# A gated-attention and pooling trunk: attention's input product as 24 steps of seven products, half of x turned beside them, W_out's sums moved into mixing

## What is computed

```python
h = x @ w_in                                   # 2048 x 1024 by 1024 x 3088
q, k, v, g, lr = split(h, [512, 1024, 2048, 3072])
gk = log_sigmoid(lr @ w_gk + b_gk) / 16        # lr: 16 columns
b = cumsum(gk within a chunk)
qe, ke, kd = q * exp(b), k * exp(-b), k * exp(b_last - b)
o = tril(qe @ ke.T) @ v + qe @ S               # S: state, decayed per chunk
o = rms_norm(o) * norm_w * silu(g)
x = layernorm(ALPHA * x + o @ w_out)
# layer 1: u, z = x @ w_in; m = (pool(u) - u) @ w_grp + b; x = layernorm(ALPHA * x + (m * scale * silu(z)) @ w_out)
```

## Time and profile before

| | us |
|---|---|
| median of three runs | 2002.89 |
| the profiled execution | 2001.48 |
| its span in the profile | 1999.6 |
| prepare | 0 to 132.3 |
| project, first to last matmul | 135.3 to 690.7 |
| attention | 692.8 to 1002 |
| mixing, with its first turns from 1009 | to 1999.6 |

### The profile page before, as it was taken

One profiled execution on the slowest core, in us unless ns is written; L12 is line 12 of the kernel. 1 busy time (PEld: TensorE's weight loads), 2 busy tenths in 40 slices (PEclk: granted clock), 3 DMA queues, 4 the chain that ended last, 5 costly groups with the idle time before them and its releaser, 6 DMA issues.

```text
span 1999.6 us, 24456 instructions
## 1 busy us (share of the span) xinstructions
PE 1914.5 (96%) x8974; PEld 1588.5 (79%) x8974; DVE 1161.7 (58%) x1539; ACT 701.3 (35%) x1065; POOL 431.5 (22%) x268
## 2 busy tenths in 40 slices
PE   8999999999999989999949999999999999999997
PEld 7778887888888778888738888887888886787786
DVE  4330102332415277787675688868678657546998
ACT  4441213131313243343354444344434335224331
POOL 0005200000000000000043666423334343322430
PEclk9999999999999999999979999999999999999999
DMA  8766530334233464455322444333322225647342
GB/s 254 221 202 239 178 103 17 108 87 118 79 101 87 159 242 164 172 187 170 136 96 74 153 141 152 135 104 137 129 88 73 94 74 193 249 170 272 129 177 95
DMA packets 229912, 287.74 MB, mean 144 GB/s; under 512 B 17216, under 2 KB 170176, under 8 KB 227904
## 3 DMA queue, kind: packets, MB, share of 16 engines
q1 hardware_dynamic: 225216, 278.20, 42.0%
q10 hardware_dynamic: 4608, 8.39, 1.1%
HBM read 186.93 MB, written 99.61 MB: 143 GB/s over the span
## 4 chain that ended last, share of the span: by engine, by line
PE 41%; DVE 4%; issue 4%; ACT 1%; POOL 0%; DVEq 0%; POOLq 0%; ACTq 0%
PE banks L165 13%; PE banks L166 13%; PE banks L167 13%; DVE m_w_lo L1922 1%; DVE m_x_lo L1936 1%; ACT m_x_hi L1728 0%; DVE m_x_lo L1914 0%; PE banks L1621 0%; PE banks L1668 0%; DVE m_stats L2025 0%; DVE m_x_lo L1896 0%; DVE m_res L2019 0%; DVE m_res L2035 0%; POOL m_s L1859 0%; DVE m_win_b L1968 0%
## 5 line engine op out<-in xcount | busy, mean ns | idle before, releaser
L165 PE MATMUL banks<-m_x_hi,m_w_hi 128*128 128x512 f32 x1320 | 517.6, 392 | 9.4 <-DVE m_res L2019 3.5
L166 PE MATMUL banks<-m_x_lo,m_w_hi 128*128 128x512 f32 x1320 | 515.3, 390 | 0.0
L167 PE MATMUL banks<-m_x_hi,m_w_lo 128*128 128x512 f32 x1320 | 515.0, 390 | 0.0
L165 PEld LDWEIGHTS banks<-m_x_hi,m_w_hi 128*128 128x128 f32 x1320 | 248.7, 188 | 63.7 <-DVE m_w_lo L1922 10.0
L166 PEld LDWEIGHTS banks<-m_x_lo,m_w_hi 128*128 128x128 f32 x1320 | 248.8, 188 | 52.0 <-issue 0.7
L167 PEld LDWEIGHTS banks<-m_x_hi,m_w_lo 128*128 128x128 f32 x1320 | 248.7, 188 | 52.0
L1854 POOL TENSOR_TENSOR m_s<-pair_raw 128x512 f32<-128x512 f32 x24 | 47.3, 1969 | 891.6 <-POOLq L947 757.5
L165 PE MATMUL banks<-x_hi,h_w_hi 128*128 128x512 f32 x512 | 199.9, 390 | 0.8 <-DVE h_g_out L833 0.8
L166 PE MATMUL banks<-x_lo,h_w_hi 128*128 128x512 f32 x512 | 199.3, 389 | 0.0
L167 PE MATMUL banks<-x_hi,h_w_lo 128*128 128x512 f32 x512 | 199.3, 389 | 0.0
L1716 ACT ACTIVATE m_w_hi<-m_s 128x512 fp32r<-128x512 f32 x184 | 115.5, 629 | 202.7 <-PE banks L167 179.2
(11 more groups left out here) (220 smaller groups left out, 3117.7 us busy)
## 6 DMA issues: line engine op xcount, KB each, us to landing
p_in<-in_pool_w_in SPq DMA_DIRECT2D x32, 256.0 KB, 4.9
p_rows<-in_x SPq DMA_DIRECT2D x16, 512.0 KB, 5.2
w_fused<-p_out SPq DMA_DIRECT2D x32, 256.0 KB, 3.9
h_out_rows<-in_pool_w_out SPq DMA_DIRECT2D x16, 512.0 KB, 6.7
v_tiles<-v_out ACTq DMA_DIRECT2D x32, 256.0 KB, 2.1
w_terms<-h_out_terms SPq DMA_DIRECT2D x8, 1024.0 KB, 5.6
h_raw<-in_gla_w_in SPq DMA_DIRECT2D x16, 512.0 KB, 4.2
g_tiles<-h_g_out SPq DMA_DIRECT2D x32, 256.0 KB, 2.3
```

The costliest lines, as they stand in the source:

```text
L165: nc.tensor.matmul(out, a_hi, b_hi, start=first, stop=False, skip_group_check=True)
L166: nc.tensor.matmul(out, a_hi, b_lo, start=False, stop=False, skip_group_check=True)
L167: return nc.tensor.matmul(out, a_lo, b_hi, start=False, stop=last, skip_group_check=True)
```

## The change

`project` becomes 24 steps of seven products, with the order of mixing. Steps 0 to 7 form v for two token tiles at a time: the stationary quarters are tiles of x, loaded from a new DRAM copy of x turned (`x_in`), the moving ones the seven terms of v's weights (`b_hi`, `b_lo`). Steps 8 to 15 and 16 to 23 form q with k, or a pair of gate columns, for the first and the second half of the tokens; there the moving terms are the seven terms of x. The elementwise work of a head is done in two halves of 1024 tokens at places given by tables. x's terms are formed by VectorE in the v steps (`x_terms`), stored, and loaded again into v's buffers as these come free. `prepare` turns only the first half of x and stores it, and forms v's terms on GpSimd, ScalarE and VectorE; the second half is turned in `project`. The sums of W_out move to GpSimd in mixing. `w_fused` is now stored in rows of 2048 columns. ScalarE's and VectorE's lists are written in slots, one behind each product of the step; a table such as `ENDS_AT` names for each head the step of the epoch and the slot, as (7, 3). In the new `prepare` GpSimd's sums wait for all four loads, and ScalarE's step 18 for all sixteen sums.

```diff
         z_src = self.a["pool_w_in"][0].rearrange("(k p) c -> p k c", p=P)
-        sp.dma_start(raw[:, 0:KT, :], self.w_fused[m]).then_inc(self.pair_loaded[s], DMA)
+        u_src = self.w_fused.rearrange("(k p) c -> p k c", p=P)
+        sp.dma_start(raw[:, 0:KT, :], u_src[:, :, m * P:(m + 1) * P]).then_inc(self.pair_loaded[s], DMA)
         sp.dma_start(raw[:, KT:2 * KT, :], z_src[:, :, m * P + POOL_W:(m + 1) * P + POOL_W]
                      ).then_inc(self.pair_loaded[s], DMA)
 
...
-    p.at = p.stream_at
+    V_LOADS = {1: (0, 0), 7: (0, BLK), 3: (HALF_K, BLK), 2: (HALF_K, 0)}
+    V_LOADS_AT = {10: 1, 12: 7, 14: 3, 16: 2}
+    FIRST_PART = 18
+    PAIR_AT = 26
...
         def x_tile(n):
 
-            return n // 2 if n % 2 else None
+            return n // 4 if n % 4 == 1 else None
...
                     if n >= 2:
                         store(n - 2)
+                    if x_tile(n) is not None and x_tile(n) >= 1:
+                        store_x(x_tile(n) - 1)
+                    if n in V_LOADS_AT:
+                        load_values(V_LOADS_AT[n])
+                    if n == PAIR_AT:
+                        load_first_pair()
                     if n % KT == 0 and n // KT + 1 < GROUPS:
                         load_grp(n // KT + 1)
                     if n == TILES // 2:
                         load_columns()
-                    if n == TILES - 4:
-                        p.prefetch_values(sp)
                 for n in (TILES - 2, TILES - 1):
...
+                b11, b12, b22, b21 = (p.b_raw[j] for j in V_LOADS)
+                for j in V_LOADS:
+                    pool.wait_ge(b_loaded[j], DMA)
+                for k in range(HALF_K):
+                    at = 4 * k
+                    nc.gpsimd.tensor_tensor(p.b_raw[5][:, k, :], b12[:, k, :], b11[:, k, :], ALU.subtract
+                                            ).then_inc(b_summed, 1)
+                    pool.wait_ge(b_summed, at + 1)
+                    nc.gpsimd.tensor_tensor(p.b_raw[6][:, k, :], b22[:, k, :], p.b_raw[5][:, k, :], ALU.subtract
+                                            ).then_inc(b_summed, 1)
+                    nc.gpsimd.tensor_tensor(p.b_raw[7][:, k, :], b22[:, k, :], b12[:, k, :], ALU.subtract
+                                            ).then_inc(b_summed, 1)
+                    pool.wait_ge(b_summed, at + 2)
+                    nc.gpsimd.tensor_tensor(p.b_raw[4][:, k, :], b21[:, k, :], p.b_raw[6][:, k, :], ALU.subtract
+                                            ).then_inc(b_summed, 1)
...
+                        if t >= 2:
+                            act.wait_ge(p.x_in_stored[t % 2], t // 2 * DMA)
+                        nc.scalar.activation(x_out[t % 2][:], x_ps[t % 2], ACT.Copy).then_inc(x_copied, 1)
                     if n >= 1:
                         copy_out(n - 1)
+                    if n >= FIRST_PART:
+                        act.wait_ge(b_summed, 4 * HALF_K)
+                        j, rows = ORDER[(n - FIRST_PART) // 2], slice((n - FIRST_PART) % 2 * 2, (n - FIRST_PART) % 2 * 2 + 2)
+                        nc.scalar.activation(p.b_hi[j][:, rows, :], p.b_raw[j][:, rows, :], ACT.Copy).then_inc(b_hi_done, 1)
                 copy_out(TILES - 1)
 
             @block.vector
...
-                                                ).then_inc(x_lo, 1)
+                    if n >= FIRST_PART:
+                        j, rows = ORDER[(n - FIRST_PART) // 2], slice((n - FIRST_PART) % 2 * 2, (n - FIRST_PART) % 2 * 2 + 2)
+                        dve.wait_ge(b_hi_done, n - FIRST_PART + 1)
+                        nc.vector.tensor_tensor(p.b_lo[j][:, rows, :], p.b_raw[j][:, rows, :],
+                                                p.b_hi[j][:, rows, :].bitcast(F32), ALU.subtract)
         for s in held:
             nc.gpsimd.sem_clear(s)
             nc.release_semaphore(s)
...
+    GATE_AT = {0: (1, 1), 1: (3, 5), 2: (5, 2), 3: (6, 5)}
+    ABS_AT = {0: (1, 1), 1: (3, 5), 2: (5, 2), 3: (6, 5)}
+    LN_AT = {0: (1, 2), 1: (4, -1), 2: (5, 3), 3: (7, -1)}
+    SUB_AT = {0: (1, 3), 1: (4, 0), 2: (5, 4), 3: (7, 0)}
+    SCAN_AT = {0: (1, 5), 1: (4, 1), 2: (5, 5), 3: (7, 1)}
+    EXPS_AT = {0: (2, 0), 1: (4, 2), 2: (6, -1), 3: (7, 2)}
+    ENDS_AT = {0: (2, 1), 1: (4, 3), 2: (6, 0), 3: (7, 3)}
+    Q_AT = {0: (3, -1), 1: (4, 4), 2: (6, 0), 3: (7, 4)}
+    KEYS_AT = {0: ((3, 1), (3, 0)), 1: ((4, 5), (5, -1)), 2: ((6, 2), (6, 1)), 3: ((7, 5), (8, -1))}
+    TURN_KEYS_AT = {0: (3, 3), 1: (5, 0), 2: (6, 4), 3: (8, 0)}
+    SILU_AT = {0: (1, 4), 1: (2, 4), 2: (5, 4), 3: (8, 5)}
+    NORM_AT = {0: (2, -1), 1: (3, 2), 2: (6, -1), 3: (9, -1)}
+    LATE_P5 = (STEP_OF["qk", 1], STEP_OF["qk", 3])
+    TURN_HI = {0: (0, 3), 1: (0, 4), 2: (0, 5), 3: (1, -1), 4: (1, 0), 5: (1, 1), 6: (1, 2)}
+    TURN_LO = {0: (0, 4), 1: (0, 5), 2: (1, -1), 3: (1, 0), 4: (1, 1), 5: (1, 2), 6: (1, 3)}
...
+            def load_x(e, n):
+
+                sp.wait_ge(product_mm, 7 * (e * EPOCH - 1) + n + 1)
+                sp.dma_start(x_raw[ORDER[n]][:], p.x_in[e - 1, (0, 1, 3, 7, 4, 5, 6)[ORDER[n] - 1]]
+                             ).then_inc(x_loaded[n], DMA)
...
+            store_k(2 * HEADS - 1, 1)
+            store_kn(2 * HEADS - 1)
+            store_gates(2 * HEADS - 1)
+            sp.wait_ge(q_stored, 2 * HEADS * 2 * DMA)
+            sp.wait_ge(k_stored, 2 * HEADS * 4 * DMA)
+            sp.wait_ge(kn_stored, 2 * HEADS * 2 * DMA)
...
+            for s in range(2):
+                p.load_qkv(sp, s, s)
...
+            def product(i, n):
+                j = ORDER[n]
+                pe.wait_ge(w_lo_done, PRODUCTS * i + n + 1)
+                if i and i % EPOCH == 0:
+                    pe.wait_ge(x_lo_done, turns_to(i // EPOCH, n))
...
+            for i in range(STEPS):
+                for n in range(PRODUCTS):
+                    product(i, n)
+                    if i < HALF_K and n in (1, 4):
+                        turn_x(KT + 2 * i + n // 4)
+                    for m in due(TURN_KEYS_AT, i, n):
+                        turn_keys(m)
+                    for m in due(GATE_AT, i, n):
+                        gate_rows(m)
+                if i and i % EPOCH == 0:
+                    rank_rows(i)
+            turn_keys(2 * HEADS - 1)
...
+            copy_keys(2 * HEADS - 1)
+            silu_of(2 * HEADS - 1)
...
+            keys_of(2 * HEADS - 1, 1)
+            norm_of(2 * HEADS - 1)
...
+            def x_terms(i, part):
+
+                r = raws[i % 2]
+                b11, b21, b12, b22 = (r[:, q * HALF_K:(q + 1) * HALF_K, :].rearrange("p k t -> p (k t)") for q in range(4))
+                t1, t2, t3, t4 = (terms[:, n, :] for n in range(4))
+                if part == 0:
+                    dve.wait_ge(pair_loaded[i % 2], 2 * (i // 2 + 1) * DMA)
+                    dve.wait_ge(terms_stored, i * DMA)
+                    nc.vector.tensor_tensor(t1, b12, b11, ALU.subtract).then_inc(x_summed, 1)
+                    nc.vector.tensor_tensor(t3, b22, b12, ALU.subtract).then_inc(x_summed, 1)
+                else:
+                    dve.wait_ge(x_summed, 4 * i + 1)
+                    nc.vector.tensor_tensor(t2, b22, t1, ALU.subtract).then_inc(x_summed, 1)
+                    dve.wait_ge(x_summed, 4 * i + 3)
+                    nc.vector.tensor_tensor(t4, b21, t2, ALU.subtract).then_inc(x_summed, 1)
+
...
+    OUT_CHUNKS, FIRST_OUT_CHUNK = 2 * HALF_K, MT + 1
...
+                if 0 <= i - FIRST_OUT_CHUNK - 2 < OUT_CHUNKS:
+                    store_out_terms(i - FIRST_OUT_CHUNK - 2)
...
+                if 0 <= i - FIRST_OUT_CHUNK < OUT_CHUNKS:
+                    load_out_rows(i - FIRST_OUT_CHUNK)
...
+            def out_sums(c):
+
+                b11, b12, b21, b22 = (out_rows[:, r, b * BLK:(b + 1) * BLK] for r in range(2) for b in range(2))
+                t1, t2, t3, t4 = (out_terms[:, n, :] for n in range(4))
+                pool.wait_ge(out_rows_loaded, (c + 1) * 2 * DMA)
+                if c:
+                    pool.wait_ge(out_terms_stored, c * DMA)
+                nc.gpsimd.tensor_tensor(t1, b12, b11, ALU.subtract).then_inc(out_summed, 1)
+                nc.gpsimd.tensor_tensor(t3, b22, b12, ALU.subtract).then_inc(out_summed, 1)
+                pool.wait_ge(out_summed, 4 * c + 1)
+                nc.gpsimd.tensor_tensor(t2, b22, t1, ALU.subtract).then_inc(out_summed, 1)
+                pool.wait_ge(out_summed, 4 * c + 3)
+                nc.gpsimd.tensor_tensor(t4, b21, t2, ALU.subtract).then_inc(out_summed, 1)
+
...
+                if 0 <= i - FIRST_OUT_CHUNK - 1 < OUT_CHUNKS:
+                    out_sums(i - FIRST_OUT_CHUNK - 1)
```

1110 lines of the change are left out of this document (691 added, 419 removed).

## The result

The changed kernel takes 2045.72 us (median of 4 runs, 2043.47 to 2050.43) where the kernel before takes 2003.22 (4 runs, 2000.88 to 2004.32): ratio 1.0217, 95% interval 1.0197 to 1.0237. It is slower by 42.5 us. The forecast was 1989.

A forecast was written before the change was run, and what follows sets the result against it. TensorE was taken to set the pace. Terms -54.7 (work), +11.6 (losses between), +12.6 (prepare), +16 (end of block) and +0.5 (mixing) gave -14: 1987.5 us, 1989 against the median, range 1970 to 2006.

The forecast's parts named there:

- The work that leaves, -54.7: Input product: TensorE's work falls to 492.2 us against 546.9 with seven products, -54.7 us.
- Prepare, +12.6: Prepare: TensorE stalls 18 us because ScalarE's step 18 waits for GpSimd's sixteen sums; +12.6 us net, bounds -6 and +18.
- The end of the block, +16: Before attention's first scores: last keys, norm and stores, then loads of q, k, v follow the last product; +16, bounds +10, +22.
- (a): Start of the input product: cold clock on TensorE's first matmuls, 1.6 us lost.
- (d): Input product, turning x between epochs twice: 2 us lost at the first turn, 12 at the second.
- (b): Input product's v steps: the single x row buffer is reloaded between slots, 1.5 us lost.
- (c): Input product's sixteen gate, q and k steps: VectorE's work fits, u3's add is tight; 3 us lost, bounds 0 and 24.
- The weighing beside it: Input product: GpSimd's sums delaying VectorE's passes, taken as 1 us a step, bounds 0 and 5.2.
- Mixing, +0.5: Mixing: GpSimd's 32 added sums cost nothing; w_fused stored in rows costs 0.5 us.
- the cover: Mixing: steps already having eight GpSimd operations without TensorE waits show the sums free; otherwise 8 x 2 us.
- Rival C: Input product: VectorE becomes the bound in steps with ends and keys, eight losing 3 us, turns 5 more each; 2023, chance 0.15.
- D: Rival, turns of x in the product: x's reload is late, each turn losing 6 us more; 2001, chance 0.15.

The follow-up runs named there:

- rows_first: Changed kernel with one 512 KB load of x rows issued first in the product's first step, ahead of SyncE's wait for x's terms: 2047.7 us.
- start_fix: Changed kernel, product's first step: x rows and first terms' store issued ahead of the next pair, second step's terms formed two slots later: 2045.4 us.
- wsums_short: Changed kernel with GpSimd's four weight-sum instructions a step cut to 8 columns from the input product's second step on: 2029.7 us.
- out_short: Changed kernel with GpSimd's W_out sums in chunks 1 to 7 of mixing cut to 8 columns instead of 512: 2038.7 us.
- out_dve: Changed kernel with W_out's sums formed by VectorE at the end of steps 18 to 25 of mixing instead of by GpSimd: 2035.3 us.
- combo4: The same combination of edits as combo3, but with all weight sums on GpSimd as in the changed kernel: 2001.1 us, ratio 0.9999 to the kernel before.
- combo3: Changed kernel with all edits together, column loads late, some loads reordered, weight sums on VectorE only in steps 0 to 9 and 17: 1997.5 us, ratio 0.9971.
- halves: Changed kernel, prepare splitting v's terms by halves of rows, so step 18 waits for 8 of GpSimd's 16 sums: product starts at 140.6 us, 8.3 earlier.
- halves_columns: Changed kernel with v split by halves of rows, v's loads two steps earlier and column loads at step 28 of prepare: 2037.5 us.

## Why the prediction was wrong, point by point

Of the 56 us between the forecast change of the span and the measured one, 43 lie in what the product loses between its matmuls and 11 in mixing; the terms for the work that leaves, for prepare and for the end of the block hold within 1 us.

**The work that leaves, -54.7: right.** Steps 4 to 7 take 19.04 us, v steps with two transposes 20.83, and 492.2 us of work plus the 63 lost are the 555.2 between 148.9 and 704.

**Prepare, +12.6: right in size and place.** It came out as +13.6, with 14.61 us at 95.87 where the text put 18 at 94.6, and three waits of 1.2 (109.25, 124.52 and 139.78). The mechanism is shown in part only: removing the wait for sums gives 7 to 8 us, because 10 us of waiting for a w_fused store lie ahead of it. I had taken that second stall as swallowed, which is true only while the first one stands. (The 7.0 saved by eight fewer turns is 6.5 by its own rows, 3.25 and 4.06, and enters no sum.)

**The end of the block, +16: right.** It is 19.1 us from the last product's end (704.43 to 723.51), key transposes included, instead of 2.15: +16.9. Moving one link of it wins nothing.

**What the product loses between, (a) to (d): wrong, 63 against 20.1. This is the step that turned the sign.** Four terms:
- (a) and (b), the start, 3.1 put, 14.7 measured. I priced the reload of x's row buffer but not where it stands in SyncE's list: behind a wait for VectorE's terms, which GpSimd's passes stretch from 0.69 to 1.78. rows_first and start_fix show a chain of four links (rows, terms' store, x's store, the pair), of which TensorE sees the last that is left.
- (c), gate, q and k steps: 3 for sixteen steps put, 21.8 measured, near the upper bound of 24 that I had. I looked at one margin, the third product's add, and overlooked the turn of keys in TensorE's own list, which waits for VectorE's last key (4 waits besides the long one, 5.9 us together, before the last product), and ScalarE's copy for the seed (4.3). wsums_short takes some 8 us of the 21.8 away: the rest is VectorE's and ScalarE's queue itself.
- The weighing beside it, 1 us a step for GpSimd. The text takes it, but its sum has it only in the allowance for the turns: 1.6, 1.5, 3, 2 and 12 are the 20.1, although 1 us a step is more than the margin of 0.8 that it gives the third product's add. What leaving the sums out gives back is 18.4 us over 24 steps, 0.77 a step, and it is not even: 10.2 of it fall on the turns of x and the first step, where VectorE has no slack. The row that I took against a full wait at each collision, a mean of 0.849 over 12 passes, hides ten passes of 0.68 to 0.69 and two of 1.65.
- (d), the turns of x: 2 and 12 put, 6.7 and 19.8 measured. At the first one TensorE waits for VectorE's add behind held low parts, and with GpSimd's sums cut short 5.0 of the 6.7 go. At the second one the walk of VectorE's queue was right about x_lo (0 to 4 done 20.8, 26.1, 30.8, 35.6 and 38.4 us after the step's start, where it put 19.7, 25.3, 30.5, 35.8 and 38.7); it left out that the keys stand behind it in the same queue and that a store of kn then stands before a copy into the same place of SBUF (8.4 and 7.7 us). I had named the queues and not the buffer.

**Mixing, +0.5: wrong, +11.5.** The step that failed is the cover: "GpSimd already has eight operations a step, and TensorE waits for nothing". It counts instructions. Four of those eight are of 256 columns, the new ones all of 512. GpSimd's groups of the seven steps before, from 1121 to 1261 us, and of the new sums, from 1432 to 1597:

```profile
L1872 POOL TENSOR_TENSOR m_stage_t<-m_stage_b 128x256 f32<-128x256 f32 x7 | 12.1, 1734 | 0.0
...
L2358 POOL TENSOR_TENSOR m_out_terms<-m_out_rows 128x512 f32<-128x512 f32 x8 | 14.5, 1810 | 0.0
```

VectorE's windows are not what differs: the kernel before has eight window passes a step in steps 9 and 10 beside eight GpSimd instructions and loses nothing, while step 22, with seven in its list, loses 3.4. The two steps before, and step 22 after (busy PE, PEld, DVE, ACT, POOL):

```profile
1221.20:1261.10 39.90, 39.90 (x185) 33.19 (x184) 36.02 (x36) 16.93 (x30) 25.94 (x17) 1.00 0.41 124
...
1512.90:1535.30 22.40, 19.29 (x86) 15.67 (x84) 22.13 (x18) 7.26 (x13) 18.01 (x10) 1.00 0.49 161
```

GpSimd is busy 13.0 us a step in the first and 18.0 in the second. The new sums also start late in the step, behind the landing of their own store, so that they run right up to VectorE's add of the third product (1520.66 to 1527.6, the add at 1526.44). Whether their length or their place costs more is not tested. out_short returns 6.7, out_dve 8.4 of it. In the combinations, where VectorE forms these sums, mixing takes 990.5 to 992.2 against 990.3 before, so the 0.5 put for w_fused's rows fits.

**Rival C** (VectorE becomes the bound, 2023) was the right family with a chance of 0.15 and too small a price: it had 24 us in eight steps and 10 at the turns. The 5.2 us a step named for a full wait at each sum would not have been its sum either: over 24 steps they are 125. D did not happen: the longest wait for a term of x's 7 MB at the first turn is 1.8 us, ScalarE's.

## What to carry to other kernels

Where work moves off the engine that bounds and onto two others that hold each other up, count collisions and their lengths and not instructions: with the order as it was, GpSimd passes that were cheap by themselves cost some 18 us in the product and 8 in mixing, and giving them to VectorE, the busier engine, paid in mixing and in the first step. The 18 are not a price of their own, though: with the order of stores, loads and keys mended, the same passes on GpSimd cost 3.6 (combo4 against combo3). A collision costs where the held pass stands before something that the bounding engine waits for. Before costing a step, write down for the bounding engine every wait in its own list, and behind each the buffer that the waited-for engine still needs to get back. A stall that is removed uncovers the one beneath it: look in the trace for other engines' waits under the same stretch before putting its whole length into the sum.

## What the runs showed of the hardware

- VectorE's passes with all operands in SBUF wait for a GpSimd pass and are not slowed in proportion: beside GpSimd a pass takes up to 1.1 us more whatever its own length, 0.28 becoming 1.40 (128 columns), 0.69 up to 1.8 (512), 1.24 up to 2.2 (1039) and 2.29 up to 3.4 (2048). GpSimd's 1.28 becomes some 1.7, 2.2 and 3.3 beside VectorE's passes of 0.69, 1.2 and 2.28. Passes of 512 columns with a PSUM input take 0.67 to 0.69 with or without a GpSimd pass beside them. A tensor-scalar pass with a single SBUF input of 1024 columns is held too (0.81 becomes 1.78). The Trainium skill, page "SBUF — State Buffer", section "SBUF: two separate sides", has the ports that VectorE shares with GpSimd as an exclusive lock for the whole instruction, taken by a VectorE pass with two SBUF inputs or in one of its modes with two ports. The traces agree: both kinds of pass are held, 0.69 to 1.78 and 0.81 to 1.78. By this rule rival C should have had the larger chance.
- Four loads of single elements for 4 small tensors, issued in the middle of prepare, keep SyncE from 68.12 to 74.92 in the changed kernel; the next store of w_fused goes out 12.2 us after the last one and lands 6.6 us after its issue (median 3.1), and ScalarE waits 10.1 us for it. Issued at the end of prepare, the longest such wait from 60 to 125 us is 3.0 (halves and halves_columns, which has v's loads two steps earlier as well). The kernel before, where nothing else was changed, waits 3.4 instead of 6.3 there and gains 0.15%.
- A stretch of idle TensorE can cost more than itself: in steps 22 and 24 of mixing waits of 3.1 and 3.5 us cost 3.4 and 5.4. Behind the second the mean granted clock from 1569 to 1576 is 0.76 and matmuls from 1570.6 to 1573.1 start 0.43 apart, as at 523.52; behind the first, from 1527 to 1534, it is 1.00.
